# First attention of a fused two-layer block: join factors of two heads in one reciprocal and one product, and both joins of a pair in every other step

## The reference, cut to what matters

```
def block(args):                       # i: token block
    i, qb1, qb2 = args
    mask = kpos[None, :] <= qpos[:, None]
    def probs(qb, k):
        s = jnp.einsum('bhqd,bshd->bhqs', qb, k) * scale
        return jax.nn.softmax(jnp.where(mask, s, -jnp.inf), axis=-1)
    a = probs(qb1, k1) - lam * probs(qb2, k2)
    return jnp.einsum('bhqs,bshe->bhqe', a.astype(v.dtype), v)
```

## Time and profile before

| what | value |
|---|---|
| median of 3 runs | 2317.76 us (2317.54 to 2319.17) |
| profiled execution, its own time | 2321.46 us |
| its span | 2319.7 us |
| TensorE busy | 2256.5 us (97%) |
| VectorE busy | 1512.9 us (65%) |
| ScalarE busy | 951.3 us (41%) |

### The profile page before, as it was taken

How to read it: one execution, slowest core, us unless ns; L and a number is a source line. 1 busy time by engine, 2 the same in 40 slices (tenths; PEclk the granted TensorE clock), 3 DMA queues, 4 the chain that set the end, 5 groups by cost and what they waited for, 6 DMA issues and landing times.

```text
span 2319.7 us, 29678 instructions
## 1 busy us (share of the span) xinstructions
PE 2256.5 (97%) x12574; PEld 1153.8 (50%) x12574; DVE 1512.9 (65%) x1959; ACT 951.3 (41%) x1396; POOL 202.8 (9%) x246
## 2 busy tenths in 40 slices
PE   7999999999999999999999988899999999999999
PEld 5455444444444444444544446664444444566655
DVE  6789857866766766778653268995553460677761
ACT  6255234423232323342332178772322321677750
POOL 0001021000000000352320200002100000000000
PEclk9999999999999999999999999999999999999999
DMA  5111110121112111112122010011032140001021
GB/s 193 37 37 37 37 37 21 53 73 70 39 37 73 62 48 70 40 39 110 37 73 73 1 37 1 1 73 63 11 104 114 51 132 1 1 1 37 2 92 55
DMA packets 51972, 120.16 MB, mean 52 GB/s; under 512 B 2890, under 2 KB 8579, under 8 KB 51456
## 3 DMA queue, kind: packets, MB, share of 16 engines
q1 hardware_dynamic: 48616, 105.40, 12.8%
q10 hardware_dynamic: 3224, 12.87, 1.6%
HBM read 101.49 MB, written 12.58 MB: 49 GB/s over the span
## 4 chain that ended last, share of the span: by engine, by line
PE 86%; DVE 8%; ACT 4%; DMA 1%; issue 1%; SPq 0%; DVEq 0%; ACTq 0%
PE PS L72 80%; PE PS L75 5%; ACT RG L81 2%; DVE R L93 2%; DVE R L101 1%; DVE RG L104 1%; DVE RG L101 1%; DMA RG<-in_a_w_in 1%; ACT R L81 1%; DVE oss L110 1%; DVE dg L104 1%; DVE scl L110 0%; DVE mx L110 0%; ACT OV L81 0%; DMA R<-in_x 0%
## 5 line engine op out<-in xcount | busy, mean ns | idle before, releaser
L72 PE MATMUL PS<-R,RG 128*128 128x512 f16 (+1 forms) x5568 | 1186.0, 374 | 9.2 <-DVE R L101 4.2
L72 PEld LDWEIGHTS PS<-R,RG 128*128 128x128 f16 (+1 forms) x5568 | 550.3, 103 | 637.5 <-issue 11.0
L72 PE MATMUL PS<-RG,R 128*128 128x512 f16 (+2 forms) x3080 | 601.1, 361 | 0.9 <-DVE R L93 0.5
L72 PEld LDWEIGHTS PS<-RG,R 128*128 128x128 f16 (+1 forms) x3080 | 279.3, 105 | 297.5 <-issue 15.6
L81 ACT ACTIVATE RG<-RG,scl 128x4096 f16<-128x4096 f32 (+2 forms) x70 | 177.8, 2556 | 206.8 <-DVE scl L113 206.8
L101 DVE SCALAR_TENSOR_TENSOR RG<-RG,scl 128x4096 f16<-128x4096 f32 (+2 forms) x70 | 213.0, 3050 | 71.0 <-ACT RG L81 71.0
L107 DVE TENSOR_TENSOR_SCAN RG<-RG,dg 128x128 f32<-128x128 f32 (+7 forms) x128 | 167.6, 1347 | 123.2 <-ACT RG L81 122.7
L101 DVE SCALAR_TENSOR_TENSOR R<-PS,scl,R 128x512 f32<-128x512 f32 (+1 forms) x211 | 148.5, 742 | 114.0 <-PE PS L72 107.4
L110 DVE TENSOR_REDUCE scl<-RG 128x1 f32<-128x4096 f32 (+1 forms) x35 | 150.3, 4294 | 99.8 <-DMA RG<-in_w_ff 41.2
L81 ACT ACTIVATE R<-PS,scl 128x512 f32<-128x512 f32 (+1 forms) x104 | 68.6, 686 | 265.3 <-PE PS L72 251.7
L122 POOL PARTITION_ALL_REDUCE scl<-scl x49 | 33.9, 694 | 1592.1 <-DVE scl L110 1311.2
(11 more groups left out here) (141 smaller groups left out, 1675.0 us busy)
## 6 DMA issues: line engine op xcount, KB each, us to landing
RG<-in_w_ff SPq DMA_DIRECT2D x16, 2048.0 KB, 8.5
RG<-in_a_w_in SPq DMA_DIRECT2D x8, 2048.0 KB, 8.7
xspill<-R ACTq DMA_DIRECT2D x2, 4096.0 KB, 15.8
RG<-in_w_kv SPq DMA_DIRECT2D x4, 2048.0 KB, 7.9
RG<-in_b_w_in SPq DMA_DIRECT2D x4, 2048.0 KB, 8.4
RG<-in_w_in SPq DMA_DIRECT2D x3, 2048.0 KB, 8.4
R<-in_x SPq DMA_DIRECT2D x8, 512.0 KB, 8.6
RG<-in_w_out SPq DMA_DIRECT2D x2, 2048.0 KB, 7.7
```

Source lines behind the costliest of these rows:

```text
L72: return self.engine.matmul(*a, **k) if self.engine else Nothing()
```

## The change

The factors of two groups of one head are computed together, and both joins follow in the same step. On VectorE the joins of the group v and v + 1 (v even, in blocks 2 to 7) are done in step v + 2: one reciprocal and one product over 128x2, then two joins. In odd steps no single-head join is done. Groups of four or two heads keep one factor pair for each group, in step v + 2 where it was v + 1. All that follows a join moves one step later: the transposes (`turn_a(u - 3, ...)`), their copies, the product with V (group u - 4), the squares and the gate (group u - 4), and the loop runs one step longer. `top`, `exp` and `scores` stay in their steps, and the buffers are unchanged except for the place of the factors in `oss`.

```diff
--- before.py
+++ after.py
@@ -974,17 +974,17 @@
             product_n(28, NT - 1, ("gg", NT - 1, 0), bank=6)
             scores(2)
             product_n(29, NT - 1, ("gg", NT - 1, 1), bank=7)
-            for u in range(2, N + 3):
+            for u in range(2, N + 4):
                 if u == 2:
                     scores(3)
                 if 4 <= u < N:
                     scores(u)
-                turn_a(u - 2, 0)
-                if u == N + 2:
+                turn_a(u - 3, 0)
+                if u == N + 3:
                     for i in range(4):
                         finish_turn(i, 0, i)
-                if u >= 3:
-                    v = u - 3
+                if u >= 4:
+                    v = u - 4
                     i, hs = da_groups[v]
                     for x, h in enumerate(hs):
                         if h % 4 == 0:
@@ -998,8 +998,8 @@
                             mm = e.matmul(bo[:, 128 * (h % 4):128 * (h % 4) + 128], AT[v % 2][:, at:at + 128],
                                           VV[:, j, 128 * h:128 * h + 128], start=(j == 0), stop=(j == i))
                     mm.then_inc(*full.up("pva", i, hs[-1]))
-                turn_a(u - 2, 1)
-                if u == N + 2:
+                turn_a(u - 3, 1)
+                if u == N + 3:
                     for i in range(4):
                         finish_turn(i, 1, (i + 4) % 6)
 
@@ -1952,30 +1952,45 @@
                 e.tensor_reduce(out, z, AX.X, ALU.max, negate=True).then_inc(*sig("top_a").up(u, sides[-1]))
 
             N = len(da_groups)
-            for u in range(N + 4):
+            def join_factors(v):
+                i, hs = da_groups[v]
+                n = 2 if len(hs) == 1 else len(hs)
+                at = 8 * (v // 2 % 2 if len(hs) == 1 else v % 2)
+                ri, ro = oss[:, at:at + n], oss[:, at + 4:at + 4 + n]
+                e.wait_ge(*sig("exp").at(v + 1 if len(hs) == 1 else v, 1))
+                e.reciprocal(ri, l_sum(1, i, hs[0], n)).then_inc(*step.up())
+                e.wait_ge(*step.last())
+                e.scalar_tensor_tensor(ro, l_sum(0, i, hs[0], n), lamt[:, 5:6], ri, ALU.mult,
+                                       ALU.mult).then_inc(*step.up())
+                e.wait_ge(*step.last())
+
+            def join_sides(v):
+                i, hs = da_groups[v]
+                w = width(i)
+                a, a2 = ea(v), e2(v)
+                at = 4 + (8 * (v // 2 % 2) + v % 2 if len(hs) == 1 else 8 * (v % 2))
+                for x in range(len(hs)):
+                    ax = a[:, w * x:w * x + w]
+                    join = e.scalar_tensor_tensor(ax, a2[:, w * x:w * x + w], oss[:, at + x:at + x + 1], ax, ALU.mult,
+                                                  ALU.add)
+                join.then_inc(*sig("joined_a").up(v))
+
+            for u in range(N + 5):
                 if u < da_first:
                     top(u, (0, 1))
                 elif u < N:
                     top(u, (0,))
                     top(u, (1,))
-                if 1 <= u < N + 1:
-                    v = u - 1
-                    i, hs = da_groups[v]
-                    w, n = width(i), len(hs)
-                    a, a2 = ea(v), e2(v)
-                    ri, ro = oss[:, 8 * (v % 2):8 * (v % 2) + n], oss[:, 8 * (v % 2) + 4:8 * (v % 2) + 4 + n]
-                    e.wait_ge(*sig("exp").at(v, 1))
-                    e.reciprocal(ri, l_sum(1, i, hs[0], n)).then_inc(*step.up())
-                    e.wait_ge(*step.last())
-                    e.scalar_tensor_tensor(ro, l_sum(0, i, hs[0], n), lamt[:, 5:6], ri, ALU.mult,
-                                           ALU.mult).then_inc(*step.up())
-                    e.wait_ge(*step.last())
-                    for x in range(n):
-                        ax = a[:, w * x:w * x + w]
-                        join = e.scalar_tensor_tensor(ax, a2[:, w * x:w * x + w], ro[:, x:x + 1], ax, ALU.mult, ALU.add)
-                    join.then_inc(*sig("joined_a").up(v))
-                if 3 <= u < N + 3 and da_groups[u - 3][1][-1] % 4 == 3:
-                    i, hs = da_groups[u - 3]
+                if 2 <= u < N + 2:
+                    if len(da_groups[u - 2][1]) > 1:
+                        join_factors(u - 2)
+                        join_sides(u - 2)
+                    elif u % 2 == 0:
+                        join_factors(u - 2)
+                        join_sides(u - 2)
+                        join_sides(u - 1)
+                if 4 <= u < N + 4 and da_groups[u - 4][1][-1] % 4 == 3:
+                    i, hs = da_groups[u - 4]
                     g = hs[-1] // 4
                     gg = GG[:, i, cols512(g)]
                     c0 = 8 * i + 4 * g
@@ -2003,7 +2018,7 @@
                     finish_factor()
                 if u == da_first + 11:
                     factor(31)
-                if u == N:
+                if u == N + 1:
                     finish_root(0)
                     for x in range(8):
                         finish_half(x % 4, x // 4)
@@ -2675,16 +2690,16 @@
                 ex.then_inc(*banks.empty(held, sig("exp"), u, c))
 
             N = len(da_groups)
-            for u in range(N + 4):
+            for u in range(N + 5):
                 if u == 0:
                     e.wait_ge(*sig("weight").at(30))
                 if u < N:
                     exp(u, 0)
                 if u == N:
                     finish_root(0)
-                turned(u - 2, 1)
-                if 3 <= u < N + 3 and da_groups[u - 3][1][-1] % 4 == 3:
-                    i, hs = da_groups[u - 3]
+                turned(u - 3, 1)
+                if 4 <= u < N + 4 and da_groups[u - 4][1][-1] % 4 == 3:
+                    i, hs = da_groups[u - 4]
                     g = hs[-1] // 4
                     bo = banks.ap(("pva", i, g))
                     e.wait_ge(*full.at("pva", i, hs[-1]))
@@ -2704,10 +2719,9 @@
                     gate_silu(NT - 1)
                     e.wait_ge(*sig("table").at())
                     e.activation(lamt[:, 7:8], epst[:, 0:1], ACT.Exp)
-                    turned(0, 0)
                 if u >= 2:
-                    turned(u - 1, 0)
-                for x in {N + 1: range(4), N + 2: range(4, 8)}.get(u, ()):
+                    turned(u - 2, 0)
+                for x in {N + 2: range(4), N + 3: range(4, 8)}.get(u, ()):
                     finish_high(x % 4, x // 4)
             finish_root(1)
             convert(31)
```

## The result

The changed kernel takes 2332.31 us (median of 6 runs), the one before 2317.86 (6 runs): ratio 1.0056, with a 95% interval of [1.0045, 1.0067], that is 10 to 16 us slower. One of the six runs, of 5982 us, is left out of the ratio. The profiled execution took 2332.28 us.

The account below looks back on a forecast made before the run. The prediction took a closed ring of maxima, exponentials and scores through three engines as the bound, not VectorE's sum. Terms 0.2 + 1.7 + 2.4 + 1.9 + 1.1 + 3.1 = +10.4 us gave 2328.2 us, range 2320.5 to 2333.

Parts of the forecast that it names:

- The step is a ring, VectorE's 94% is no bound: Attention steps: maxima, exponentials, scores, next maxima close a loop, 4.04 us in block 6; two joins make even steps 4.74.
- The gate must wait for the squares: Odd gate steps, blocks 4 to 7: VectorE waits for ScalarE's squares; block 6 next maxima at 4.6 us against 4.04.
- Sums of blocks 4, 5, 6, 7: Step lengths added up per block, after against before: +0.2, +1.7, +2.4 and +1.9 us.
- Steps 0 to 21: Early steps (2 to 21 in the prediction): longer blocks 2 and 3, a better start; +1.1 us, from -2 to +3.
- The drain: After the last maxima: one more loop step of 3.65 us, partly covered by ScalarE's table load; +3.1 us.
- From the profiled execution to the median: Whole kernel: profiled 2321.46 plus 10.4 gives 2331.9; 3.7 taken off, as the runs' median lay lower: 2328.2 us.
- VectorE's sum: Rival: VectorE's total work is the bound, so all 10.8 us of factors come back, 2307 us; chance 0.07.
- no change: Rival: steps borrow from one another, the average of even and odd steps stays the same, 2318 us; chance 0.06.
- small losses: Rival: squares ready in time, drain covered, early steps even; +3.4 us, 2321 us; chance 0.13.
- Longer waits: Rival: squares delay side 1's exponentials, 0.5 us in each of 11 gate steps; +15.9, 2333.7 us; chance 0.08.

Follow-up runs that it names:

- e2: Changed kernel with one join in each step, the second join of a pair one step later, factors still in pairs: 2318.30 us, ratio 0.9997 to the kernel before.
- e3: Changed kernel without ScalarE's squares and the wait for them, outputs not normalized: 2314.55 us, ratio 0.9981 to the kernel before.
- e4: Kernel before the change without ScalarE's squares and the wait for them, outputs not normalized: 2312.25 us, ratio 0.9972.
- e9: Changed kernel timed and traced once more, nothing altered: 2331.84 us, ratio 1.0053 to the kernel before.
- e7: Changed kernel with 34 extra transposes into a free bank, 17 in step 4 and 17 in the drain: 2330.23 us, ratio 1.0050 to the kernel before.
- e1: Changed kernel's one-step delay alone, each join single with its own factors, one per step: 2320.47 us, ratio 1.0005 to the kernel before.
- e8: Kernel before with the gate in three pieces from block 4 on, its sum of squares halved over the two following steps: 2316.43 us, ratio 0.9988.
- e5: Kernel before with the gate's sum of squares (0.60 us) one step later from block 4 on: 2315.27 us, ratio 0.9985.
- e6: e2 with the gate's sum of squares two steps later, from the last gate of block 3 on: 2315.40 us, ratio 0.9986 to the kernel before.

## Why the prediction was right, and where it was not

Forecast 2328.2 (+10.4), measured 2332.3 (+14.5), 0.3 over the 2324 to 2332 that the forecast gave itself. The mechanism of the steps held; the drain and the way from one execution to the median came out too small. Step by step, as the prediction put them:

- *The step is a ring, VectorE's 94% is no bound.* Right. The even steps came at 4.73 and 5.26 (forecast 4.74 and 5.27), plain odd ones at 4.03 and 4.43 (4.04, 4.44): a late start is never made up. e2 shows the freed 0.45 us as idle time.
- *The gate must wait for the squares.* Right: odd gate steps 4.54 in block 6 and 4.89 in block 7 (forecast 4.58 and 4.87), with the wait ahead of the gate's product; e3 and e4 put it at 3.9 us in after, at none in before. In step 21 of block 3 the wait is 1.82 us; before, in step 20, 0.73.
- *Sums of blocks 4, 5, 6, 7.* +0.25, +2.11, +2.19, +1.83 for +0.2, +1.7, +2.4, +1.9. The 0.4 in block 5 is step 33, 5.63 us for a forecast of 5.25: I had put the single reduction and the small operations behind its gate and let the maxima follow at once; in the trace these wait another 0.31 us, as the scores of group 34 are late too. Timeline of VectorE, beside the earlier trace rows:

```profile
1457.59 0.69 DVE L93 TENSOR_TENSOR R<-PS,R 128x512 f32<-128x512 f32 x1 [1.04 <-ACT OV L81]
...
1458.79 0.67 DVE L110 TENSOR_REDUCE scl<-R 128x1 f32<-128x512 f32 x1
...
1460.22 1.02 DVE L104 CUSTOM_DVE_ANT_0 RG<-PS,scl 128x768 bf16<-128x768 f32 x1 [0.31 <-PE PS L72]
```

- *Steps 0 to 21, +1.1.* +1.27, and +1.31 in e9, and right in its parts: steps 0 to 5 are 0.8 us shorter (forecast 1 to 1.5), block 2 is 0.6 longer and block 3 1.4 (forecast 0.7 and 1.4).
- *The drain, +3.1.* The step that failed: mis-sized, it measured +5.03. One drain step of 3.65 less some cover was right (+3.25 with the filler, e7; +3.6 in e1, whose clock stayed up). What I had not costed is a stretch of the drain at half the clock: 1.8 us of the last part by e7, 1.3 of them where the clock is down. TensorE's waits there are no longer than before's 2.16 us (1.38 and 0.57), so they alone don't explain it.
- *From the profiled execution to the median.* The traces differ by 10.7 us in span, close to the forecast +10.4: 12.7 from the first maxima on, less 2.0 that the profiled execution of after was ahead by then (1338.89 for 1340.87), in stages that the change doesn't touch; other traces start the maxima anywhere from 1336.7 to 1341.1. I took off 3.7 us because before's profiled execution stood so far above its median. After's stood at its median (2332.28 and 2332.31), so that what came off was these 2.0 and not 3.7. So the missing 4.1 us are 2.3 of the sum (12.7 for 10.4, the drain above all) and 1.7 of this step. That the spans differ by nearly the forecast is luck, an early start of after's execution against a drain that was too small. And 2317.86 lies low for before: beside the experiments its medians were 2318.53, 2319.28 and 2318.99 (69 runs in all), and e9 is 12.85 us over the last, near the 12.7 of the traces.

*VectorE's sum*, *no change* and *small losses* fell with the steps. *Longer waits*, 2333.7, is nearer than the forecast by the number but not by the mechanism: its 0.5 us more in each gate step are not there.

The trace shows three of four steps of before with VectorE idle, and work regrouped there changed the time in both directions. The Trainium skill (Perfetto Trace Analysis, Optimizing Scalar/DVE Operations) says that where an engine is not saturated but makes others wait, breaking up instructions may let work be completed sooner. No run here shows a gain from breaking one up: e8, which halves the reduction, is 0.1 us from e5 in blocks 4 to 7. What gained is to take apart two instructions that stood in a row (e5, 1 to 6 us faster than before).

What stays open: which waits of TensorE are followed by the lower clock. e1 has one of 1.52 us in the same place as after's and its next product takes 2.05 us, without a drop.

## What to carry to other kernels

A busy share of 94% does not make an engine the bound: where it idles ahead of the instruction that closes the loop of the step, work taken off is worth nothing in that step, and work moved in costs its full time beyond the idle time. So spread operations over the steps that have slack, and take apart what stands in a row (here the gate's two instructions), as long as the pieces land where there is slack (e8 shows the end of it). A delay by one step costs about one step of the drain (here 3.3 to 3.8 us for a step of 3.65); subtract that first.

## What the runs showed of the chip

- Waits of TensorE of 1 to 2 us were followed by a stretch at 0.50 in some traces and not in others: behind 1.38 and 0.57 us in the drain of after and again in e9 but not behind 1.38 alone in e3, behind 1.94 us at the start of after, e2 and e9 but not of e1, e3 and e6, behind 2.16 us in e4 but not in before. Timeline of TensorE and the clock there, in after:

```profile
1357.47 0.66 PE L75 MATMUL PS<-ident,RG 128*128 128x128 f32 x4 [1.94 <-DVE RG L101]
```

```profile
1358.00:1360.00 2.00, 2.00 (x18) 1.25 (x16) 1.72 (x5) 1.97 (x7) 0.00 (x0) 0.72 0.00 0
1360.00:1362.00 2.00, 2.00 (x15) 1.48 (x14) 1.20 (x2) 1.79 (x7) 0.00 (x0) 0.50 0.00 0
```

The Trainium skill (Perfetto Trace Analysis, Matmul Optimizations) says that this engine scales power with its utilization and that matmuls should execute back to back in batches; e7, which fills the wait of the drain with transposes nobody reads, is in line with it (1.8 us in one trace), and the equal waits with and without a drop show that the wait's length alone does not decide it.

- Such drops also come without the change (e4 has them at 1358 to 1362 and 1542 to 1546), and the spread between runs goes with the mean clock: before took 2316.9 to 2319.7 us at 0.999 (43 runs), 2318.3 to 2321.4 at 0.998 (19) and 2320.7 to 2325.0 at 0.996 to 0.997 (7).
- A reciprocal of two columns takes as long as one of one column (0.16 us), and so does the product (0.22): pairing them is free on VectorE, and 24 pairs (16 of them in blocks 4 to 7) saved 9.6 us of its time, of which 1.5 us reached the end of blocks 4 to 7 (e1 to e2).
